# Convolution layer's input projection: twelve of sixteen channel blocks by seven half-size block products instead of eight full ones, on one Trainium2 core

## The chip, the cores and the metric

The kernel is one program on one core of a Trainium2 chip. The metric is the device time of one execution in microseconds. Five instruction streams run side by side: TensorE (PE, with its weight loads shown as PEld), VectorE (DVE), ScalarE (ACT), GpSimd (POOL) and SyncE (SP), which issues nearly all transfers.

## The reference, cut to what matters

A stack of layers on 512 tokens of width 1024 in float32: pool mixer, convolution mixer, latent attention, pool mixer, and then two blocks with attention and a feed-forward layer. The change touches the convolution mixer:

```
xn = rms_norm(x, conv_norm)                      # 512 x 1024
b, c, h, z = split(xn @ w_in, 4)                 # w_in: 1024 x 8192, so 4 parts of 2048 channels
y = b * causal_depthwise_conv(c * h, conv_w)     # width 3 along the tokens
x = x + (y * silu(z)) @ w_out                    # w_out: 2048 x 1024
```

## The kernel before, in words

**Products.** Tokens lie on the free axis, channels on the partitions. Every float32 operand is split into a high part (rounded to fp32r, by ACT) and a low part (the rest, by DVE or POOL), and each product is three matmuls: high by high, high by low, low by high (`mm3`, L454 to L456). A *unit* is a weight tile of 128x1024 for one block of 128 output channels: `gemm8` runs 8 steps of k, so 24 matmuls of 512 columns.

**Weights.** The units form one long list (`unit_table`), and every engine walks it in the same order. SP loads a unit into one of four `raw` buffers; ACT copies it to `WH` (L1133); DVE subtracts to get `WL` (L1837), or POOL does, in pieces of 256 columns (L2707), where the unit's last field says so; TensorE then multiplies. `WH` and `WL` are rings of three, so ACT can write unit n only when TensorE is done with unit n-3. The calls `weights(n)` and `taking(key)` in each engine's program fix where in its order of work this split takes place; `taking` goes two units ahead (`LOOK = 2`). All orders are written out by hand; a queue waits at each `wait_ge` with everything behind it.

**Convolution.** `conv_layer` exists in each engine's program and loops over 16 blocks of 128 channels. A block has four units, cc, ch, cb and cz (c, h, b and z). DVE scales c by 1/rms squared (L1968) and multiplies by h (L1974); ACT makes the first tap (L1251), DVE the two others (L1978, L1981), POOL multiplies by 1/rms (L2759); DVE multiplies b (L1988) and scales z (L1866); ACT takes silu (L1257), POOL multiplies it in (L2764), ACT and DVE split the result into `YH` and `YL` (L1142, L1845). After 8 blocks an output projection of 8 units follows (`out_proj("co", ...)`). The position angles for the later attention (DVE, L2032 to L2050) and their sines (ACT) lie in blocks 1 to 5.

**Other work that is named later.** The feed-forward layers at the end already use a seven-product scheme, in `quarter`, from which the names Q1 to Q7 and W5 come. `v_part` in the attention has matmuls of 256 columns.

Of the kernel before, what the change touches and what calls it, by code (L numbers as in the profile page):

```python
# [15 lines left out]
S = 512  # L16
# [55 lines left out]

FF_ORDER = (0, 4, 1, 5, 2, 6, 3, 7)
# [12 lines left out]
SEMS = ("xin0", "xin1", "xin2", "xin3", "xin4", "xin5", "xin6", "xin7", "consts", "vec", "raw0", "raw1", "raw2", "raw3", "pos", "lam", "cos", "sin", "fn", "out",  # L86
# [48 lines left out]
def unit_table(D):  # L135

    units, index, lows = [], {}, False

    def add(key, src, ncol, dup=False):
        index[key] = len(units)  # L140
        units.append([src, ncol, dup])
# [22 lines left out]
    for i2 in range(8):  # L164
        for i in (2 * i2, 2 * i2 + 1):
            for off, nm in ((16, "cc"), (32, "ch"), (0, "cb"), (48, "cz")):
                add((nm, i), D["conv_in"][0, off + i], 1024)
        if i2 % 4 == 3:
            out_units("co", D["conv_out"], i2 // 4)
# [28 lines left out]
    for l in range(2):  # L198
# [10 lines left out]
        for qd in range(4):  # L209
            for i in FF_ORDER:  # L210
                add(("f1", l, qd, i), D[f"ff1{l}"][0, qd * 8 + i], 1024)
                if qd == 0 and i == 0:
                    low(False)
            for name in PRODUCTS:
                for kk in range(2):
                    add(("zq", 4 * l + qd, name, kk), (4 * l + qd, name, kk), 1024)
    for n, u in enumerate(units):
        on = False
        for at, now in flips:
            if at + (0 if now else 0) <= max(n - LOOK, 0):  # L220
                on = now
        u.append(on)
    loaded = [n for n, u in enumerate(units) if not isinstance(u[0], tuple)]
    slots = {n: (i % NRAW, loaded[i - NRAW] if i >= NRAW else None) for i, n in enumerate(loaded)}
    return units, index, slots
# [75 lines left out]
def program(nc, D, out):  # L301
    ctx = ExitStack()
    with ctx:
# [26 lines left out]
        raw = [sb(f"raw{i}", WN) for i in range(NRAW)]  # L330
# [18 lines left out]
        units, unit, slots = unit_table(D)  # L349
# [63 lines left out]
        def weight_source(n):  # L413
            src, ncol = units[n][0:2]
            if isinstance(src, tuple):
# [15 lines left out]
        def pe_program(handle, c):  # L431
# [146 lines left out]

            def conv_layer():
                for i2 in range(8):  # L580
                    for i in (2 * i2, 2 * i2 + 1):
                        xgemm(1, "cc", i, first=i == 0)
# [530 lines left out]
        def act_program(handle, c):  # L1113
# [127 lines left out]
            def conv_layer(done):  # L1241
                for i2 in range(8):
                    for i in (2 * i2, 2 * i2 + 1):
                        taking("cc", i)
                        if i == 0:
                            root(1, 1024)
                        taking("ch", i)
                        act.wait_ge(*at("ch", i))
                        if i > 1:
                            act.wait_ge(*at("cb", i - 2))  # L1250
                        act.do.activation(CV[i % 2], temp("ch", i), ACT.Copy, scale=vcol("conv_w2", i)).then_inc(  # L1251
                            *mark("act", ("cv2", i)))
                        taking("cb", i)
                        taking("cz", i)
                        t = temp("cz", i)
                        act.wait_ge(*at("czr", i))
                        act.do.activation(t, t, ACT.Silu).then_inc(*mark("act", ("czs", i)))  # L1257
                        y_high("co", i // 8, i % 8, t, ("czy", i))
                        if i == 5:
                            sines()  # L1260
                    if i2 % 4 == 3:
                        out_proj("co", i2 // 4, done if i2 == 7 else None)

# [548 lines left out]
        def dve_program(handle, c):  # L1812
# [64 lines left out]
            def out_proj(name, rb, st=None, first=0):  # L1877
                for m in range(first, 8):
                    taking(name, rb, m)
                    add_out(m, (name, rb, m), ("x", name, rb, m) if st is None else ("x", st, m))  # L1880
                    if st is not None and st != "mid" and st < 8:
# [76 lines left out]
            def conv_layer():  # L1958
                for i2 in range(8):
                    for i in (2 * i2, 2 * i2 + 1):  # L1960
                        taking("cc", i)
                        if i == 0:
                            recip_root(1, R[:, :])
                            dve.wait_ge(*mine())
                            dve.do.tensor_tensor(CR2, R[:, :], R[:, :], ALU.mult).then_inc(*mark("dve", ("r2",)))
                        dve.wait_ge(*at("mm", "cc", i))
# [9 lines left out]
                        a = CV[i % 2]  # L1976
                        dve.wait_ge(*at("cv2", i))
                        dve.do.scalar_tensor_tensor(a, shifted(("ch", i), 1), vcol("conv_w1", i), a, ALU.mult,  # L1978
                                                    ALU.add).then_inc(*mark("dve"))
                        dve.wait_ge(*mine())  # L1980
                        dve.do.scalar_tensor_tensor(a, shifted(("ch", i), 2), vcol("conv_w0", i), a, ALU.mult,  # L1981
                                                    ALU.add).then_inc(*mark("dve", ("cv0", i), ("tfree", "ch", i)))
                        taking("cb", i)
                        dve.wait_ge(*at("mm", "cb", i))
                        dve.wait_ge(*at("cv", i))
                        if i > 1:
# [6 lines left out]
                        low(YL[i % 8][:, :], t, YH[i % 8][:, :], ("yh", "co", i // 8, i % 8),  # L1993
                            ("yl", "co", i // 8, i % 8), ("tfree", "cz", i))
                        if i == 1:
                            positions()
                        if i == 2:
                            angle("sin", SIN[:, :], 0.0, 0.0)
                        if i == 3:
                            angle("cos", COS[:, :], 0.25, math.pi / 2)  # L2000
                    if i2 % 4 == 3:
                        out_proj("co", i2 // 4, 2 if i2 == 7 else None)
# [677 lines left out]
        def pool_program(handle, c):  # L2680
# [72 lines left out]
            def conv_layer():  # L2753
                for i2 in range(8):
                    for i in (2 * i2, 2 * i2 + 1):
                        taking("ch", i)
                        pool.wait_ge(*at("cv0", i))
                        pool.wait_ge(*at("rstd", 1))
                        pool.do.tensor_tensor(CV[i % 2], CV[i % 2], R[:, :], ALU.mult).then_inc(*mark("pool", ("cv", i)))  # L2759
                        taking("cz", i)  # L2760
                        t = temp("cz", i)
                        pool.wait_ge(*at("czs", i))
                        pool.wait_ge(*at("cb", i))
                        pool.do.tensor_tensor(t, t, CB[i % 2], ALU.mult).then_inc(*mark("pool", ("czy", i)))  # L2764
                        if i == 6:
                            pool.wait_ge(*at("sin"))
                            pool.do.tensor_scalar(SIN[:, :], SIN[:, :], const[:, C_SGN:C_SGN + 1], None,
                                                  ALU.mult).then_inc(*mark("pool", ("sinr",)))
                    if i2 % 4 == 3:
# [374 lines left out]
```

## Time and profile before

| | |
|---|---|
| Time, median of 3 runs | 2676.91 us (2676.52 to 2676.93) |
| The profiled execution | 2678.12 us, of which the span of the core is 2676.3 |
| Granted TensorE clock, mean | 0.998 |
| TensorE busy | 2652.0 us, 99% of the span |
| DVE, ACT, POOL busy | 64%, 48%, 24% |
| The convolution layer | from 315.9 us, blocks of 21.8 us; the first output projection is issued from 462.3 |

The page gives busy time over the whole program. TensorE being busy in nearly all of it says that the other engines are hidden now; how much room each has is to be read in the stretch that is changed.

### The profile page before, as it was taken

How to read it: one execution, taken by the hardware profiler on the slowest of the kernel's cores; microseconds unless marked ns; L12 is line 12 of the kernel's file. 1: busy time of each engine (PE TensorE's matmuls, PEld its weight loads, DVE VectorE, ACT ScalarE, POOL GpSimd, SP SyncE). 2: the span in 40 equal slices, each digit the busy share in tenths (PEclk: the TensorE clock that was granted, in tenths of full speed). 3: DMA queues.
4: the chain of work that ended last, by engine and by line, in shares of the span. 5: the costliest groups of instructions: out<-in, count | busy, mean ns of one | idle time of the engine just before them, and what ended most of it. 6: DMA issues, size and time to landing. Idle time of an engine off the chain costs nothing.

```text
span 2676.3 us, 32512 instructions
## 1 busy us (share of the span) xinstructions
PE 2652.0 (99%) x12772; PEld 2222.6 (83%) x12772; DVE 1703.9 (64%) x2604; ACT 1272.0 (48%) x2002; POOL 651.6 (24%) x688
## 2 busy tenths in 40 slices
PE   8999999999999999999999999999999999999998
PEld 7888888888888888888888888788888888788887
DVE  7656554344466646666574768776677468776677
ACT  4323332222346636533235677654445677654445
POOL 1000111011126626500003744420000554420000
PEclk9999999999999999999999999999999999999999
DMA  4222222222221222222222221354551221255540
GB/s 161 98 99 98 90 103 102 95 95 95 96 68 63 68 88 66 79 87 105 95 100 97 79 72 40 105 141 148 173 158 42 80 64 48 97 152 153 173 142 32
DMA packets 76841, 263.98 MB, mean 99 GB/s; under 512 B 8976, under 2 KB 11536, under 8 KB 76688
## 3 DMA queue, kind: packets, MB, share of 16 engines
q1 hardware_dynamic: 71568, 245.12, 26.7%
q0 software_dynamic: 5120, 16.78, 3.7%
q8 instruction: 101, 1.65, 0.2%
q14 instruction: 52, 0.43, 0.0%
HBM read 259.77 MB, written 2.10 MB: 98 GB/s over the span
## 4 chain that ended last, share of the span: by engine, by line
PE 91%; DVE 4%; ACT 2%; POOL 2%; issue 0%; DMA 0%; SPq 0%; ACTq 0%; DVEq 0%
PE ps L454 27%; PE ps L455 26%; PE ps L456 26%; PE ps L460 2%; PE ps L459 2%; PE ps L461 2%; POOL wl L2707 2%; PE ps L595 1%; PE ps L857 1%; PE ps L856 1%; DVE wl L1837 1%; ACT wh L1133 0%; DVE xl L1849 0%; PE ps L528 0%; ACT xh L1144 0%
## 5 line engine op out<-in xcount | busy, mean ns | idle before, releaser
L454 PE MATMUL ps<-xh,wh 128*128 128x512 f32 x1920 | 752.2, 392 | 0.1
L455 PE MATMUL ps<-xl,wh 128*128 128x512 f32 x1920 | 748.1, 390 | 0.0
L456 PE MATMUL ps<-xh,wl 128*128 128x512 f32 x1920 | 748.0, 390 | 0.0
L1133 ACT ACTIVATE wh<-raw 128x1024 fp32r<-128x1024 f32 (+3 forms) x389 | 397.6, 1023 | 474.4 <-PE ps L456 434.9
L454 PEld LDWEIGHTS ps<-xh,wh 128*128 128x128 f32 x1920 | 361.0, 188 | 77.0 <-issue 1.2
L456 PEld LDWEIGHTS ps<-xh,wl 128*128 128x128 f32 x1920 | 360.9, 188 | 75.3
L455 PEld LDWEIGHTS ps<-xl,wh 128*128 128x128 f32 x1920 | 361.0, 188 | 74.7 <-issue 1.0
L1837 DVE TENSOR_TENSOR wl<-raw,wh 128x1024 fp32r<-128x1024 f32 (+1 forms) x275 | 339.6, 1235 | 119.9 <-ACT wh L1133 119.9
L2707 POOL TENSOR_TENSOR wl<-raw,wh 128x256 fp32r<-128x256 f32 x408 | 315.3, 806 | 405.5 <-ACT wh L1133 405.5
L454 PE MATMUL ps<-yh,wh 128*128 128x512 f32 x640 | 251.1, 392 | 1.5 <-POOL wl L2707 1.5
L456 PE MATMUL ps<-yh,wl 128*128 128x512 f32 x640 | 249.2, 389 | 0.0
L455 PE MATMUL ps<-yl,wh 128*128 128x512 f32 x640 | 249.1, 389 | 0.0
L2716 POOL TENSOR_TENSOR acc<-acc,t 128x512 f32<-128x512 f32 x52 | 72.9, 1403 | 679.7 <-ACT t L1154 677.4
L1133 ACT ACTIVATE wh<-a 128x1024 fp32r<-128x1024 f32 x96 | 101.9, 1062 | 126.8 <-PE ps L456 64.4
L1845 DVE TENSOR_TENSOR yl<-t,yh 128x512 fp32r<-128x512 f32 (+1 forms) x148 | 101.5, 687 | 78.2 <-ACT yh L1142 78.2
L454 PEld LDWEIGHTS ps<-yh,wh 128*128 128x128 f32 x640 | 120.2, 188 | 28.6 <-POOL wl L2707 3.2
L456 PEld LDWEIGHTS ps<-yh,wl 128*128 128x128 f32 x640 | 120.1, 188 | 25.2
L1142 ACT ACTIVATE yh<-t 128x512 fp32r<-128x512 f32 (+1 forms) x148 | 86.4, 585 | 114.3 <-DVE t L1949 56.3
L455 PEld LDWEIGHTS ps<-yl,wh 128*128 128x128 f32 x640 | 120.2, 188 | 23.9
L1874 DVE TENSOR_TENSOR x<-ps,x 128x512 f32<-128x512 f32 x96 | 65.6, 688 | 116.9 <-PE ps L456 116.9
L1837 DVE TENSOR_TENSOR wl<-a,wh 128x1024 fp32r<-128x1024 f32 x96 | 117.3, 1221 | 32.1 <-ACT wh L1133 32.1
L2827 POOL DMA_DIRECT2D wsum<-in_ff2t x32 | 27.2, 976 | 328.7 <-DMA wsum<-in_ff2t 322.8
(307 smaller groups left out, 4755.3 us busy)
## 6 DMA issues: line engine op xcount, KB each, us to landing
raw<-in_pool_in SPq DMA_DIRECT2D x64, 512.0 KB, 3.2
raw<-in_conv_in SPq DMA_DIRECT2D x64, 512.0 KB, 3.2
raw<-in_ff SPq DMA_DIRECT2D x64, 512.0 KB, 6.2
a<-in_ff2t SPq DMA_DIRECT2D x64, 512.0 KB, 6.9
raw<-in_pool_out SPq DMA_DIRECT2D x32, 512.0 KB, 3.2
raw<-in_qk SPq DMA_DIRECT2D x32, 512.0 KB, 3.5
raw<-in_pool_grp SPq DMA_DIRECT2D x16, 512.0 KB, 3.2
raw<-in_conv_out SPq DMA_DIRECT2D x16, 512.0 KB, 3.2
```

Source lines behind the costliest of these rows:

```text
L454: pe.do.matmul(o, lh, rh_, start=start, stop=False)
L455: pe.do.matmul(o, lh, rl_, start=False, stop=False)
L456: return pe.do.matmul(o, ll, rh_, start=False, stop=stop)
L459: pe.do.matmul(o, lh, rh_, start=False, stop=False, skip_group_check=True)
L460: pe.do.matmul(o, lh, rl_, start=False, stop=False, skip_group_check=True)
L1133: act.do.activation(h[:, 0:ncol], r[:, 0:ncol], ACT.Copy).then_inc(*mark("whi", ("whi", k)))
L1142: act.do.activation(dst, src, ACT.Copy).then_inc(*mark("act", done))
L1837: dve.do.tensor_tensor(lo[:, 0:ncol], r[:, 0:ncol], f(h[:, 0:ncol]), ALU.subtract).then_inc(*mark("wlo", ("wlo", k)))
L1845: dve.do.tensor_tensor(dst, src, f(h), ALU.subtract).then_inc(*mark("dve", *done))
L1874: dve.do.tensor_tensor(x[m][:, :], ps(*key)[:, :], x[m][:, :], ALU.add).then_inc(*mark("dve", ("psfree",) + key, *done))
L2707: p = pool.do.tensor_tensor(lo[:, cc], r[:, cc], f(h[:, cc]), ALU.subtract)
L2716: pool.do.tensor_tensor(ACC[:, :], ACC[:, :], temp("sq", use, k), ALU.add).then_inc(*mark("pool", ("acc", use, k), ("tfree", "sq", use, k)))
```

## The change

Blocks 2 to 6 and 8 to 14 (`CONV_BLOCKS`) are computed by `conv_part` instead of four calls of `gemm8`. The four projections of a block form two pairs, (c, h) and (b, z). The input is halved along k and along the tokens, a pair's weights are halved along k, and the 2x2 block product takes seven products of half size: each has 4 steps of k with three matmuls of 256 columns, 12 matmuls. The seven are grouped into four units for each pair (`CONV_PARTS`): three of 1024 columns with two products and one of 512 with one. The units of the pairs alternate: U0 = (pair 0, part 0), U1 = (pair 1, part 0), U2, ... U7. Of the weights only part 0 and part 3 are loaded; the middle parts are four sums of 512 columns that POOL makes (`w_sums`), for block i+1 while block i runs. Four sums of the inputs for each of four k are made once, by POOL, ACT and DVE, in blocks 0 and 1 (`x_scaled`, `t_sums`, `t_high`, `t_low`). Partial sums leave PSUM through ACT and DVE (`first_sum`, `second_sums`, `third_sum`, `upper`, `lower`). The low half of part 3 (U6 and U7) is made by POOL. The rest of a block's elementwise work moves to the next block's order. Two more raw buffers are used from block 3 on. The angles move into the first output projection, the sines behind it.

```diff
+CONV_BLOCKS = (2, 3, 4, 5, 6, 8, 9, 10, 11, 12, 13, 14)
+CONV_PAIRS = ((16, 32), (0, 48))
+CONV_PARTS = (("Q1", "Q2"), ("Q6", "W5"), ("Q7", "Q3"), ("Q4",))
...
+    tails = {index["cp", i, p, 3] for i in CONV_BLOCKS for p in range(2)}
...
-        u.append(on)
+        u.append(on or n in tails)
...
+            def conv_part(i, p, j):
+                n = unit["cp", i, p, j]
+                wh, wl = unit_ready(n)
...
+                for c, name in enumerate(CONV_PARTS[j]):
...
+                    for k in range(4):
...
+                            mm = mm3(o, wh[:, cc], wl[:, cc], xh, xl, k == 0, k == 3)
```

ACT's part of `conv_layer`:

```diff
+                def x_scaled(k):
+                    if k:
+                        act.wait_ge(*at("tcs", k - 1))
+                    for dst, m in ((COS, k), (SIN, k + 4)):
+                        act.wait_ge(*at("x", 1, m))
+                        a = act.do.activation(dst[:, :], x[m][:, :], ACT.Copy, scale=vcol("conv_norm", m))
...
+                def t_high(k):
+                    if k == 0:
+                        act.wait_ge(*at("mm", "grp", 0, 3, 3))
+                    high(TC[k][:, 0:1024], RX[k % 2][:, :], ("tcs", k), ("tch", k))
...
+                def eight(i):
...
+                    if i == 1:
+                        t_high(1)
+                        x_scaled(2)
+                    taking("ch", i)
...
+                    tap(i)
+                    if i == 1:
+                        t_high(2)
+                        x_scaled(3)
+                    taking("cb", i)
+                    if i == 0:
+                        x_scaled(0)
+                    taking("cz", i)
+                    if i == 0:
+                        t_high(0)
+                        x_scaled(1)
+                    if i == 1:
+                        t_high(3)
+                    gate(i)
+                    y_out(i)
```

DVE's part:

```diff
+                def seven(i):
+                    late = i - 1 in CONV_BLOCKS
+                    for s in range(8):
+                        if late and s == 0:
+                            lower(i - 1, 1, 1)
+                            lower(i - 1, 1, 0)
+                        if late and s == 1:
+                            taps(i - 1)
+                        if late and s == 2:
+                            gated(i - 1)
+                        if s == 5:
+                            third_sum(i, 0)
+                            upper(i, 0)
+                            both_scaled(i)
+                        if s == 6:
+                            third_sum(i, 1)
+                            lower(i, 0, 1)
+                        if s == 7:
+                            lower(i, 0, 0)
+                            upper(i, 1)
+                        weights(unit["cp", i, s % 2, s // 2] + LOOK)
+                        if late and s == 4:
+                            y_out(i - 1)
```

POOL's part:

```diff
+                def w_sums(i, p):
...
+                    pool.do.tensor_tensor(s1, b[:, 0:512], b[:, 512:1024], ALU.add).then_inc(
+                        *mark("pool", ("ws1", i, p)))
...
+                    if before is not None:
+                        pool.wait_ge(*at("wlo", unit["cp", before, p, 2]))
+                    pool.do.tensor_tensor(s3, a[:, 0:512], b[:, 0:512], ALU.add)
+                    pool.wait_ge(*at("ws1", i, p))
+                    pool.do.tensor_tensor(s2, s1, a[:, 0:512], ALU.add).then_inc(*mark("pool", ("ws", i, p, 0)))
+                    pool.wait_ge(*at("ws", i, p, 0))
+                    pool.do.tensor_tensor(s4, s2, a[:, 512:1024], ALU.add).then_inc(*mark("pool", ("ws", i, p, 1)))
+
+                for i in range(16):
+                    if i - 1 in CONV_BLOCKS:
+                        taps(i - 1)
+                        gated(i - 1)
+                    if i not in CONV_BLOCKS:
+                        taps(i)
+                    if i < 2:
+                        t_sums(2 * i)
+                    if i == 1:
+                        t_sums(3)
+                    if i not in CONV_BLOCKS:
+                        gated(i)
+                    if i == 0:
+                        t_sums(1)
+                    if i + 1 in CONV_BLOCKS:
+                        w_sums(i + 1, 0)
+                        if i in CONV_BLOCKS:
+                            weights(unit["cp", i, 1, 3])
+                        w_sums(i + 1, 1)
+                    elif i in CONV_BLOCKS:
+                        weights(unit["cp", i, 1, 3])
```

`t_sums(k)` is five POOL operations of 256 columns. `taps` on POOL is the product by 1/rms, `gated` on POOL the product with silu(z), both of 512 columns. On DVE `taps` is two operations of 512 columns with both inputs in SBUF; `both_scaled`, `gated` and `y_out` are one such operation each, `lower` with half 1 is one of 256 columns; `third_sum`, `upper` and `lower` with half 0 read one input from PSUM.

## Rows read from the trace of the kernel before

**Rows 1.** The page: busy time of each engine, and the chain that ended last.
```profile
PE 2652.0 (99%) x12772; PEld 2222.6 (83%) x12772; DVE 1703.9 (64%) x2604; ACT 1272.0 (48%) x2002; POOL 651.6 (24%) x688
...
PE 91%; DVE 4%; ACT 2%; POOL 2%; issue 0%; DMA 0%; SPq 0%; ACTq 0%; DVEq 0%
```

**Rows 2.** One block's stretch: length; busy PE, PEld, DVE, ACT, POOL; granted clock, DMA.
```profile
425.40:447.20 21.80, 21.80 (x97) 18.05 (x97) 9.69 (x12) 6.01 (x7) 3.50 (x2) 1.00 0.26 97
```

**Rows 3.** Timeline of TensorE: start, duration; 256 columns, then 512.
```profile
1475.90 0.28 PE L456 MATMUL ps<-wh,xl 128*128 128x256 f32 x1
...
1476.14 0.28 PE L455 MATMUL ps<-wl,xh 128*128 128x256 f32 x1
...
1479.13 0.39 PE L454 MATMUL ps<-xh,wh 128*128 128x512 f32 x1
...
1479.81 0.39 PE L454 MATMUL ps<-xh,wh 128*128 128x512 f32 x1
```

**Rows 4.** Groups of instructions from 330 to 462 us: busy, mean ns | idle before.
```profile
L1837 DVE TENSOR_TENSOR wl<-raw,wh 128x1024 fp32r<-128x1024 f32 x26 | 31.7, 1221 | 4.0 <-ACT wh L1133 4.0
L1133 ACT ACTIVATE wh<-raw 128x1024 fp32r<-128x1024 f32 x25 | 26.2, 1052 | 20.0 <-PE ps L456 19.9
...
L2764 POOL TENSOR_TENSOR t<-t,s 128x512 f32<-128x512 f32 x6 | 7.8, 1292 | 37.7 <-ACT t L1257 37.7
L1981 DVE SCALAR_TENSOR_TENSOR s<-t,vec,s 128x512 f32<-128x512 f32 x7 | 5.3, 752 | 0.2
...
L1251 ACT ACTIVATE s<-t,vec 128x512 f32<-128x512 f32 x7 | 5.1, 724 | 36.5 <-DVE t L1974 36.5
```

**Rows 5.** Line L2759 alone: duration in ns, least, median, most.
```profile
L2759 POOL TENSOR_TENSOR s<-s,r x16: 2202/2211/2220, 335.2 to 700.5; 128x512 f32<-128x512 f32 x16
```

**Rows 6.** Timeline of DVE and POOL, four stretches: start, duration of the run.
```profile
418.00 1.22 DVE L1837 TENSOR_TENSOR wl<-raw,wh 128x1024 fp32r<-128x1024 f32 x1
418.16 2.22 POOL L2759 TENSOR_TENSOR s<-s,r 128x512 f32<-128x512 f32 x1 [11.76 <-DVE s L1981]
...
23.31 4.54 DVE L1837 TENSOR_TENSOR wl<-raw,wh 128x1024 fp32r<-128x1024 f32 x2 [3.00 <-ACT wh L1133]
24.68 4.33 POOL L2716 TENSOR_TENSOR acc<-acc,t 128x512 f32<-128x512 f32 x2
...
2328.80 4.44 POOL L2707 TENSOR_TENSOR wl<-raw,wh 128x256 fp32r<-128x256 f32 x5
2328.83 2.40 DVE L1849 SCALAR_TENSOR_TENSOR xl<-x,vec,xh 128x512 fp32r<-128x512 f32 x2
...
1501.46 0.68 DVE L2300 SCALAR_TENSOR_TENSOR s<-ps,s 128x512 f32<-128x512 f32 x1
...
1501.64 2.83 POOL L2707 TENSOR_TENSOR wl<-raw,wh 128x256 fp32r<-128x256 f32 x4
...
1504.44 1.29 POOL L2835 TENSOR_TENSOR x<-x,s 128x512 f32<-128x512 f32 x1
...
1505.69 2.82 POOL L2707 TENSOR_TENSOR wl<-raw,wh 128x256 fp32r<-128x256 f32 x4
```

**Rows 7.** Line L1845 with its operands in SBUF: least, median, most ns.
```profile
L1845 DVE TENSOR_TENSOR ptl<-s,pth x96: 539/558/7402, 1502.8 to 2318.9; 128x384 fp32r<-128x384 f32 x64, 128x512 fp32r<-128x512 f32 x32
```

**Rows 8.** Timelines of ACT in block 0 and of DVE in block 1.
```profile
333.43 1.99 ACT L1133 ACTIVATE wh<-raw 128x1024 fp32r<-128x1024 f32 x2
335.44 1.28 ACT L1257 ACT_TABLE_LOAD   x1
339.95 0.63 ACT L1257 ACTIVATE t<-t 128x512 f32<-128x512 f32 x1 [3.23 <-DVE t L1866]
...
349.28 0.69 DVE L1974 TENSOR_TENSOR t<-ps,s 128x512 f32<-128x512 f32 x1 [2.71 <-PE ps L456]
```

**Rows 9.** Stretches of 2 us, later in the program, with the granted clock.
```profile
1624.00:1626.00 2.00, 1.48 (x10) 1.48 (x11) 1.22 (x3) 1.94 (x5) 0.00 (x0) 1.00 0.01 4
...
1628.00:1630.00 2.00, 2.00 (x13) 1.59 (x12) 1.97 (x8) 2.00 (x6) 0.00 (x0) 0.50 0.00 0
```

More of the change, by code:

```diff
@@ L135, in unit_table, with add @@
 def unit_table(D):
-    units, index, lows = [], {}, False
-    def add(key, src, ncol, dup=False):
+    units, index, loads, wide, narrow = [], {}, [], [], []
+    def add(key, src, ncol, dup=False, load=True):
         index[key] = len(units)
+        if load and not isinstance(src, tuple):
+            loads.append(len(units))
         units.append([src, ncol, dup])
@@ L221, in unit_table @@
                 on = now
-        u.append(on)
-    loaded = [n for n, u in enumerate(units) if not isinstance(u[0], tuple)]
-    slots = {n: (i % NRAW, loaded[i - NRAW] if i >= NRAW else None) for i, n in enumerate(loaded)}
-    return units, index, slots
+        u.append(on or n in tails)
+    queue, holder, slots = list(range(NRAW)), {}, {}
+    for i, n in enumerate(loads):
+        if i in wide:
+            queue = [NRAW, NRAW + 1] + queue
+        if i in narrow:
+            queue = [q for q in queue if q < NRAW]
+        q = queue.pop(0)
+        queue.append(q)
+        slots[n] = q, holder.get(q)
+        holder[q] = n
+    return units, index, slots, loads
 def temp_table():
@@ L1253, in conv_layer @@
[L1253 to L1260, printed above, removed]
+                        if i in CONV_BLOCKS:
+                            seven(i)
+                        else:
+                            eight(i)
@@ new lines, in gated, with seven @@
+                def gated(i):
+                    o = CB[i % 2]
+                    dve.wait_ge(*at("cup", i, 1))
+                    dve.wait_ge(*at("cv", i))
+                    dve.do.tensor_tensor(o, o, CV[i % 2], ALU.mult).then_inc(*mark("dve", ("cb", i)))
+                def seven(i):
+                    late = i - 1 in CONV_BLOCKS
+                    for s in range(8):
+                        if late and s == 0:
+                            lower(i - 1, 1, 1)
+                            lower(i - 1, 1, 0)
+                        if late and s == 1:
+                            taps(i - 1)
[11 more added lines that the diff above has]
+                            upper(i, 1)
+                        weights(unit["cp", i, s % 2, s // 2] + LOOK)
+                        if late and s == 4:
+                            y_out(i - 1)
@@ L1959, in conv_layer @@
                 for i2 in range(8):
                     for i in (2 * i2, 2 * i2 + 1):
+                        if i in CONV_BLOCKS:
+                            seven(i)
+                            continue
+                        late = i - 1 in CONV_BLOCKS
                         taking("cc", i)
```

272 lines of the change are left out of this document (221 added, 51 removed).

## The prediction

> **What bounds the kernel now.** The page comes first: TensorE is busy in 2652.0 of 2676.3 us and holds 91% of the chain that ended last [rows 1], so time goes only where TensorE's work or its waits change. Next, the stretch of one convolution block, since the mean over the program says nothing of it: 21.8 us with TensorE busy throughout at the full clock (1.00), DVE busy 9.7, ACT 6.0, POOL 3.5 [rows 2]. Then TensorE's timeline for the price of a matmul, the groups for the other engines' prices, and last the timelines of DVE and POOL together. These last matter most, since the change gives POOL about five times its work there.
>
> **What TensorE gains.** A matmul of 512 columns starts 0.227 us after the one before, one of 256 columns 0.120 us [rows 3]. A block had 96 of the first (21.76 us) and gets 2 x 7 x 12 = 168 of the second (20.16 us). That is 1.6 us, and 19.2 us over twelve blocks: seven eighths of the columns, of which gain the fixed 13 ns of each matmul, now paid 168 times, takes back nearly half. The same sums are accumulated in PSUM, and transfers stay at four of 512 KB for a block; six raw buffers instead of four put them ahead, so I cost them at nothing.
>
> **What the other engines get, for each full block.** ACT: six splits of 1.05 us [rows 4], two half ones, six small copies and the three operations of before, about 12 us, hidden. DVE: six low halves of 1.22 us [rows 4] and eleven smaller operations, about 15 us. POOL: its two products of 512 columns, eight sums of 512 in `w_sums`, four pieces of 256 for U6 and U7. POOL's price is 1.29 us alone for 512 columns [rows 4], 1.25 from start to start in a run, and 0.70 for a piece of 256 [rows 6]: 10 x 1.25 + 4 x 0.70 = 15.3 us, with the wait for DVE's `gated` between POOL's two products (0.7) and small waits on its own results 16.4 us (0.4 for these, an estimate). Alone, this would fit under 20.16.
>
> **But the two do not run alone.** When DVE has two inputs in SBUF, it and POOL take turns. L2759, 512 columns like L2764 (1.29 us), takes 2.20 to 2.22 in all 16 blocks [rows 5], because DVE's low half has started 0.16 us before it [rows 6]. In runs, DVE's 1024 columns and POOL's 512 go pairwise at 2.2 us, which is nearly the sum of both alone; two DVE operations of 512 lengthen five POOL pieces from 3.5 to 4.44 us, 0.45 each [rows 6]. With one input in PSUM DVE is not slowed though POOL is at work (0.68 us) [rows 6]. So each of DVE's operations with two SBUF inputs lengthens POOL's chain: a low half by 0.92 (2.21 - 1.29), 512 columns by 0.45, 256 by about 0.2. In a block these are six low halves (5.5), two taps, `both_scaled` and `y_out` (1.8; `gated` falls in POOL's wait), and two `lower` (0.4): 7.7 us. POOL's round becomes 16.4 + 7.7 = 24.1 us, 3.9 more than TensorE's 20.16. The Trainium skill ("SBUF — State Buffer", section "Who interferes with whom") states this rule: a DVE instruction with two SBUF inputs contends with a GpSimd one that reads SBUF, whoever comes first blocks the other fully, and one with a single SBUF input does not contend. By that rule, the trace agrees (2.21 against 1.29 us), the change loses what its fewer products gain.
>
> Does TensorE wait for this round? POOL's order is `taps`, `gated`, `w_sums` pair 0, U6 and U7, `w_sums` pair 1, all in one queue. U6 and U7 stand behind the first sums, and TensorE can't finish a block without them; next block's `taps` stand behind the second sums, and DVE's `gated` and POOL's `gated` behind these. So the round sets the period from the second block of a run on. The last block of a run makes no sums for the next and the first block of the second run has its sums made under the output projection: I count no excess for blocks 6, 8 and 14. Blocks 3, 4, 5 and 9 to 13 pay 3.9 each, 31 us. Bounds: with holds only and no idle time, POOL has 12 and DVE 9 units of about 1.15 and 1.05 us, 23.2 us, excess 25 in all. If only half of DVE's operations met POOL's, the round would be 20.3 and the excess nothing. Upward, 26.5 us a round (51 in all) if turns go badly: one DVE operation of 0.56 us took 7.4 [rows 7], through POOL's whole run of ten from 1501.64 to 1509.8 [rows 6]. I take the sum of rows, since turns are the rule in them.
>
> **The entry.** In blocks 0 and 1 the sums of the inputs are made by a relay through in-order queues. One `t_sums` is five pieces of 256 columns, 3.9 us with waits on itself; one `t_high` 1.06; one `x_scaled` two operations, 1.4; a unit's split 1.05 + 1.22 with hops, 2.4 [rows 4, 6]. Times are on the clock of before, where ch of block 1 is done at 349.2 (DVE reads it at 349.28 [rows 8]); with units of 5.44 us block 1 starts at 338.3 and block 2 at 360.1.
> (1) ACT in block 0: after its two splits (333.43 on [rows 8]) and `x_scaled` it waits for `t_sums(0)`, which starts when L2759 ends (335.2 + 2.2 = 337.4 [rows 5]) and ends at 342.2 with one turn lost; `t_high(0)`, `x_scaled(1)`, the table load of 1.28 us and the silu [rows 8] end at 346.6 instead of 340.6. POOL's product, ACT's `y_out`, then cb's split: ready 350.9, wanted 349.2. Stall 1.7.
> (2) `t_sums(1)` from 348.0 to 353; `t_high(1)`, `x_scaled(2)`, cz's split: 357.5, wanted 356.3. Stall about 1.
> (3) DVE's product for ch stands behind that low half; then ACT's tap, DVE's taps, POOL's `taps` (2.2), only then `t_sums(2)`, `t_high(2)`, `x_scaled(3)` and U0's split, since ACT's `taking("cb")` is behind them: about 371.5, wanted 362.5. Stall 9.
> (4) `t_sums(3)`, `t_high(3)`, silu, POOL's product, three sums of `w_sums(2, 0)`, U2's split: 383.4, wanted 377.2. Stall 6.
> (5) Four more sums with one turn lost, U3's split: stall 3.
> Together 21 us. Bounds: 10 (steps 3 and 4 half as long, because some of it overlaps) and 26. I keep 21: every step is a queue that is written down.
>
> Smaller moves: the angles (7 us of DVE) go under an output projection in which DVE has little to do; blocks 7 and 15 are as before; nothing for either. A low granted clock is seen once, 0.50 from about 1627 on, right after 2 us in which TensorE was busy only 1.48 [rows 9]. The stalls forecast here are longer, so the clock may fall behind each; where POOL's round sets the period the slower matmuls fill time that TensorE would wait in, so I add nothing and widen the upper end.
>
> **Sum.** -19.2 + 31 + 21 = +33 us against the profiled execution's own 2678.1 (span 2676.3), the same edit of the same stretch as against the median 2676.9, which is 1.2 lower. Forecast 2710 us.
>
> **Rivals.**
> A. The turns are mostly missed, because DVE's and POOL's bursts fall apart in time: TensorE sets the period in all twelve blocks, and the entry, less its lost turns, is 10 to 15 us. Then -19.2 + 10 to 15: 2667 to 2673, faster. For it: the block has 20 us and POOL alone needs 16.4. Against: 15.3 us of POOL and some 9.5 of DVE's two-input work (9 times 1.05) don't fit in 20.16 without meeting. It decides if the measured round is under 20.5 us.
> B. Starved DVE: runs of three to five sums without a gap keep DVE out as in the 7.4 us case, and DVE's low halves come late as well; the clock halves. Rounds of 27 to 28: 8 x 7.5 = 60, entry 26: 2740 to 2750. For it that one case; against it, the median of the same line is 0.56 us and the pairs in [rows 6] take turns at the first boundary.
> C. The change doesn't do what it says: 256 columns don't go at 0.120 us when weights and inputs change this way. At 0.1295 us a block of 168 costs 21.76 again, the gain of 19.2 is gone in blocks 2, 6, 8 and 14 (6.4 us), and the others wait anyway: 2716. Against: the same widths run at 0.120 in `v_part` [rows 3].
>
> **Chances.** Forecast with its own range 2692 to 2732: 0.68, C included. A: 0.17, of which 0.13 faster and 0.04 within 0.2%. B: 0.10. The rest, 0.05, lies between A and the forecast. 0.2% is 5.4 us, about what a measurement of this kernel can tell. The range takes in the lower bounds of both terms (-19.2 + 25 + 10: 2693, and halfway to A) and most of the way to B: 2680 to 2742. Faster 0.13, same 0.06, slower 0.81.
>
> **What would show it.** The convolution's blocks on TensorE: 20.2 us in blocks 6, 8 and 14; about 24 in 4, 5 and 10 to 13, with the wait before U6 or U7 and released by POOL's L2707-like low half. POOL busy nearly all of a block, its sums at 1.25 to 2.2 us each instead of 1.29. TensorE waits of about 9 and 6 us around 362 and 377 us, released by low halves that follow ACT. Matmuls of 256 columns at 0.120 us apart. Wrong if POOL's operations keep 1.29 us while DVE works, if the waits in full blocks are under 1 us, or if the entry's relay overlaps more than the queues let me see.

## The result, and the profile after

The changed kernel takes 2727.11 us (median of 4 runs, 2724.9 to 2729.25) against 2676.92 for the kernel before, run beside it: a ratio of 1.0187, 95% interval 1.017 to 1.0205. The profiled execution has a span of 2726.5 us against 2676.3, so 50.2 us have to be found. The page of the kernel after, busy time by engine and then the chain that ended last, beside [rows 1]:

```profile
PE 2654.7 (97%) x13636; PEld 2265.7 (83%) x13636; DVE 1820.4 (67%) x2704; ACT 1343.8 (49%) x2134; POOL 877.2 (32%) x852
...
PE 82%; POOL 7%; DVE 6%; ACT 3%; issue 1%; DMA 0%; SPq 0%; POOLq 0%; ACTq 0%; DVEq 0%
```

TensorE's share of the chain has fallen from 91% to 82%, POOL's has risen from 2% to 7%. The end of block 1 (first line), blocks 2 to 6 and block 8, beside [rows 2] (same columns), say where:

```profile
352.00:372.20 20.20, 11.52 (x49) 8.89 (x49) 6.90 (x9) 8.13 (x10) 10.01 (x11) 0.91 0.15 52
372.20:409.90 37.70, 26.21 (x169) 25.51 (x170) 18.62 (x19) 11.96 (x18) 29.44 (x23) 0.78 0.23 80
409.90:433.90 24.00, 22.08 (x171) 21.61 (x170) 18.90 (x20) 11.46 (x17) 20.36 (x14) 0.93 0.26 90
433.90:460.30 26.40, 22.67 (x170) 22.47 (x169) 19.27 (x20) 11.26 (x17) 22.68 (x17) 0.88 0.28 86
460.30:483.20 22.90, 20.81 (x170) 20.40 (x169) 16.98 (x20) 11.47 (x17) 18.67 (x13) 0.99 0.22 73
483.20:503.40 20.20, 20.20 (x171) 20.20 (x170) 17.84 (x19) 10.87 (x16) 14.10 (x9) 1.00 0.37 126
568.90:589.05 20.15, 20.15 (x169) 20.15 (x168) 10.41 (x13) 9.71 (x14) 12.19 (x10) 1.00 0.21 68
```

Blocks 6 and 8 (the last two lines), in which TensorE waits for nothing, take 20.2 us, as computed. Block 2 takes 37.7; blocks 3, 4 and 5 take 24.0, 26.4 and 22.9; blocks 9 to 13, by the starts of their first matmuls, 26.25, 26.09, 22.91, 26.11 and 26.1. Over 20.16 each that is 12.85 + 26.7 = 39.5 us. The entry (blocks 0 to 2) is 12.1 us to the start of block 2 and 17.5 in it, 29.6. With -19.2 for the matmuls the sum is 49.9 of the 50.2 measured.

TensorE's longest waits up to block 4, from its timeline, the last figure in brackets being the idle time and what ended it:

```profile
372.17 0.58 PE L490 MATMUL ps<-xh,wh 128*128 128x256 f32 x1 [8.17 <-DVE wl L1998]
...
386.31 0.58 PE L495 MATMUL ps<-tc,wh 128*128 128x256 f32 x1 [6.77 <-DVE wl L1998]
...
405.41 0.39 PE L495 MATMUL ps<-tc,wh 128*128 128x256 f32 x1 [4.17 <-POOL wl L2959]
...
429.23 0.39 PE L495 MATMUL ps<-tc,wh 128*128 128x256 f32 x1 [1.92 <-POOL wl L2959]
...
455.05 0.58 PE L495 MATMUL ps<-tc,wh 128*128 128x256 f32 x1 [3.73 <-POOL wl L2959]
```

The first two, before block 2 and before its U2, stand in the entry. The other three are at U6 of blocks 2, 3 and 4, all ended by POOL's low half. Where the first matmul lasts 0.58 us instead of 0.39, the granted clock is already at its lower level: it is 0.50 for 3.4 to 10.2 us at nine of TensorE's waits in the layer.

POOL's round, from its timeline (the lines of the kernel after: L3009 is `taps`, L3015 `gated`, L3041 to L3050 `w_sums`, L2959 the low halves of U6 and U7):

```profile
415.51 2.21 POOL L3009 TENSOR_TENSOR s<-s,r 128x512 f32<-128x512 f32 x1 [2.61 <-DVE s L2128]
418.59 2.15 POOL L3015 TENSOR_TENSOR t<-t,s 128x512 f32<-128x512 f32 x1 [0.87 <-DVE s L2175]
420.69 2.27 POOL L3041 TENSOR_TENSOR sw<-raw 128x512 f32<-128x512 f32 x1
...
440.31 2.21 POOL L3009 TENSOR_TENSOR s<-s,r 128x512 f32<-128x512 f32 x1 [2.61 <-DVE s L2128]
```

24.8 us from one `taps` to the next; the eight blocks 3 to 5 and 9 to 13 last 25.1 in the mean. The products and sums of 512 columns that take 1.29 us alone [rows 4] have means of 1.49 to 2.21 us in these groups, the costliest of the stretch from 410 to 484 us:

```profile
L3048 POOL TENSOR_TENSOR sw<-sw,raw 128x512 f32<-128x512 f32 x4 | 8.0, 2011 | 0.0
...
L3041 POOL TENSOR_TENSOR sw<-raw 128x512 f32<-128x512 f32 x4 | 7.1, 1774 | 0.0
L3009 POOL TENSOR_TENSOR s<-s,r 128x512 f32<-128x512 f32 x3 | 6.6, 2212 | 8.5 <-DVE s L2128 8.5
L3015 POOL TENSOR_TENSOR t<-t,s 128x512 f32<-128x512 f32 x3 | 6.4, 2145 | 2.6 <-DVE s L2175 2.6
L3050 POOL TENSOR_TENSOR sw<-sw,raw 128x512 f32<-128x512 f32 x4 | 6.0, 1492 | 0.3
```

That is three rounds. The last two numbers of L3009 and L3015 matter as much: POOL stands idle (8.5 + 2.6) / 3 = 3.7 us a round, waiting for DVE. An engine that idles 3.7 us of 25 doesn't set a period by its own queue. The chain of waits shows what does: a ring, in which each step releases the next and the last one releases the first step of the next round (start, duration, what):

```profile
455.05 0.58 PE ps L495
...
458.07 1.07 ACT wh L1210
...
459.16 2.00 DVE wl L1998
461.16 1.43 DVE t L2163
...
462.92 1.13 DVE wl L1998
...
464.75 0.77 DVE s L2128
...
465.59 2.23 POOL s L3009
...
467.84 0.70 DVE s L2175
...
468.68 1.04 POOL t L3015
...
470.79 2.27 POOL sw L3041
...
477.72 3.93 POOL wl L2959 x4
```

U6 on TensorE gives a `WH` buffer back, ACT can then split the second unit of the next block, DVE makes its low half, the two `lower`, the low half of U2 and the taps, all ahead of POOL's `taps`; POOL's sums follow, and behind them the low half of the next U6. POOL's second sums run beside DVE's part of this ring, and what they have left over is POOL's idle time.

### The profile page after: what moved, and what is told of

The parts are those of the page before. It is cut to its first block, busy times and chain, and to the rows that moved or that the text cites. A ratio compares the mean times of both kernels' runs of the same rounds, so it can differ in the third digit from the quotient of the medians.

```text
span 2726.5 us, 34706 instructions
## 1 busy us (share of the span) xinstructions
PE 2654.7 (97%) x13636; PEld 2265.7 (83%) x13636; DVE 1820.4 (67%) x2704; ACT 1343.8 (49%) x2134; POOL 877.2 (32%) x852
## 3 DMA queue, kind: packets, MB, share of 16 engines
q8 instruction: 108, 1.77, 0.3%
## 4 chain that ended last, share of the span: by engine, by line
PE 82%; POOL 7%; DVE 6%; ACT 3%; issue 1%; DMA 0%; SPq 0%; POOLq 0%; ACTq 0%; DVEq 0%
PE ps L490 23%; PE ps L491 23%; PE ps L492 23%; PE ps L495 3%; PE ps L497 3%; PE ps L496 3%; POOL wl L2959 2%; DVE wl L1998 2%; PE ps L672 1%; POOL sw L3041 1%; ACT wh L1210 1%; POOL s L3009 1%; POOL sw L3048 1%; POOL sw L3046 1%; POOL sw L3050 1%
## 5 line engine op out<-in xcount | busy, mean ns | idle before, releaser
L490 PE MATMUL ps<-xh,wh 128*128 128x512 f32 (+1 forms) x1728 | 658.3, 381 | 10.9 <-DVE wl L1998 10.8
L491 PE MATMUL ps<-xl,wh 128*128 128x512 f32 (+1 forms) x1728 | 653.5, 378 | 0.0
L492 PE MATMUL ps<-xh,wl 128*128 128x512 f32 (+1 forms) x1728 | 653.2, 378 | 0.0
L1210 ACT ACTIVATE wh<-raw 128x1024 fp32r<-128x1024 f32 (+3 forms) x369 | 369.8, 1003 | 468.0 <-PE ps L492 364.5
L2959 POOL TENSOR_TENSOR wl<-raw,wh 128x256 fp32r<-128x256 f32 x440 | 344.9, 816 | 410.1 <-ACT wh L1210 410.0
L490 PEld LDWEIGHTS ps<-xh,wh 128*128 128x128 f32 x1728 | 326.7, 189 | 73.9 <-DVE wl L1998 12.0
L1998 DVE TENSOR_TENSOR wl<-raw,wh 128x1024 fp32r<-128x1024 f32 x239 | 305.5, 1279 | 122.3 <-ACT wh L1210 121.0
L492 PEld LDWEIGHTS ps<-xh,wl 128*128 128x128 f32 x1728 | 326.2, 189 | 60.5
L491 PEld LDWEIGHTS ps<-xl,wh 128*128 128x128 f32 x1728 | 326.7, 189 | 59.5 <-issue 1.0
L2006 DVE TENSOR_TENSOR yl<-t,yh 128x512 fp32r<-128x512 f32 (+1 forms) x148 | 108.6, 735 | 54.0 <-ACT yh L1219 54.0
L1219 ACT ACTIVATE yh<-t 128x512 fp32r<-128x512 f32 (+1 forms) x148 | 86.3, 585 | 112.3 <-DVE t L2112 56.4
```

The lines of the kernel that those rows point to most:

```text
L490: pe.do.matmul(o, lh, rh_, start=start, stop=False)
L491: pe.do.matmul(o, lh, rl_, start=False, stop=False)
L492: return pe.do.matmul(o, ll, rh_, start=False, stop=stop)
L1210: act.do.activation(h[:, 0:ncol], r[:, 0:ncol], ACT.Copy).then_inc(*mark("whi", ("whi", k)))
L1219: act.do.activation(dst, src, ACT.Copy).then_inc(*mark("act", done))
L1998: dve.do.tensor_tensor(lo[:, 0:ncol], r[:, 0:ncol], f(h[:, 0:ncol]), ALU.subtract).then_inc(*mark("wlo", ("wlo", k)))
```

## The experiments

**1. Take the turns away.** DVE's low halves of U0 to U5 read a spare PSUM bank instead of the raw weights or sums, so that DVE has one SBUF input. The true low halves are left out.

```diff
+                    elif k in conv_units:
+                        for c0 in (0, 512):
+                            p = dve.do.tensor_tensor(lo[:, c0:c0 + 512], PS[SPARE][:, :], f(h[:, c0:c0 + 512]),
+                                                     ALU.subtract)
```

> Changed computation: in blocks of seven products DVE's low half of U0 to U5 subtracts from a PSUM bank that nobody writes in place of the raw weights, in two operations of 512 columns, so DVE's time stays (2 x 0.61 against 1.22 us) and only one input is in SBUF. Theory 1 (turns between DVE and POOL): the round of POOL loses 5.5 us, from about 25 to 19.5, TensorE sets the period of 20.2 us in blocks 3 to 5 and 9 to 13, and their waits before U6 or U7 (0.9 to 4.6 us) vanish with the clock's drops behind them: about 40 us less, 2687 us; POOL's sums go at 1.25 to 1.3 us. Theory 2 (POOL's own work and the order of its queue are too long, whoever runs beside it): unchanged, 2727 us.

Measured: 2683.17 us (2681.92 to 2683.89), ratio 1.002 (1.0011 to 1.003). The same groups of POOL as above, in this kernel:

```profile
L3020 POOL TENSOR_TENSOR s<-s,r 128x512 f32<-128x512 f32 x4 | 5.2, 1306 | 10.6 <-DVE s L2139 10.6
L3026 POOL TENSOR_TENSOR t<-t,s 128x512 f32<-128x512 f32 x4 | 5.2, 1300 | 3.5 <-DVE s L2186 3.5
...
L3052 POOL TENSOR_TENSOR sw<-raw 128x512 f32<-128x512 f32 x4 | 5.2, 1295 | 0.0
```

POOL's operations of 512 columns are back at 1.29 to 1.33 us in the mean (these three took 2.21, 2.15 and 1.77 in the kernel after), POOL has exactly as many operations in the whole program (852), blocks 3 to 5 and 9 to 13 take 20.16 us, and 44 us are gone. DVE's own work has not become shorter than it was alone: a low half is 2 x 0.68 us, against 1.22 for the real one outside a turn. The turns between DVE and POOL are the cause of the rounds. What is left is the entry, 11.7 us ahead of block 2 and 33.9 - 20.16 = 13.7 in it, less the 19.2: 6.2 us, and the spans differ by 5.0.

**2. Make the sums once.** POOL makes the weight sums of block 2 only; later blocks use them again, so their own sums are left out.

```diff
                 def w_sums(i, p):
+                    if i != CONV_BLOCKS[0]:
+                        return
```

> Changed computation: POOL makes the sums of the weights for block 2 alone and all later blocks use these, so eight POOL operations of 512 columns are left out in each of ten blocks. Theory 1 and theory 2 both: POOL's round falls by more than 10 us, blocks 3 to 5 and 9 to 13 run at 20.2 us, 2687 us, and what is left over 2657.7 (2676.9 - 19.2) is the entry, about 29 us with block 2. A rival in which the seven-product blocks are held by ACT, by DVE's own sums or by transfers: still 24 to 26 us a block.

Measured: 2682.14 us (2679.41 to 2682.7), ratio 1.0017 (1.0007 to 1.0026). Blocks at 20.16 again, though POOL's two products still take 2.21 and 2.15 us. So turns alone cost nothing; they cost where POOL has eight sums a block to make in them. Block 2 takes 31.8 us here: without sums for block 3 its wait before U6 is gone.

**3. DVE makes the low halves of U6 and U7.** This part of the change undone.

```diff
-        u.append(on or n in tails)
+        u.append(on)
```

> The low halves of U6 and U7 go back to DVE, all else is kept. By turns: POOL's chain loses 2.8 us and meets two more DVE operations of 512 columns (0.9), so the round falls by about 1.9, eight times, and with fewer drops of the clock some 20 us in all: about 2707 us. TensorE's wait then moves from U6 to the middle units, whose sums come last. Rival: the second part of the title is what makes the block fit (DVE is the fuller engine): slower than 2727, by the 0.6 us of each DVE operation that delays U0's low half, 5 to 15 us.

Measured: 2710.18 us (2708.64 to 2711.93), ratio 1.0122 (1.0107 to 1.0137). The round is 23.43 us. Giving these low halves to POOL costs 17 us instead of sparing any: they stand in POOL's part of the ring. POOL's idle time a round is now 3.28 + 0.87 us. Of the 17 us 4.3 are in block 2, and the granted clock, which falls at six waits in the rounds of the kernel after, falls at none here, so not all of the rest is POOL's work. The size was as expected, the place of TensorE's waits was not: they are before U7 and before U0, not at the middle units.

```profile
448.81 0.35 PE L495 MATMUL ps<-tc,wh 128*128 128x256 f32 x1 [1.24 <-DVE t L2142]
452.02 0.39 PE L490 MATMUL ps<-xh,wh 128*128 128x256 f32 x1 [1.54 <-DVE wl L1998]
```

**4. Fill TensorE's wait.** 20 matmuls of 256 columns on data at hand, ahead of U6, keep TensorE at work while it waits, so that the clock isn't lowered.

```diff
+                if j == 3 and p == 0 and i + 1 in CONV_BLOCKS:
+                    b = bank("fill", i)
+                    for r in range(FILL):
+                        mm = pe.do.matmul(b[:, 0:256], XH[0][:, 0:128], XH[0][:, 0:256], start=r == 0, stop=r == FILL - 1)
```

> Added work: 20 matmuls of 256 columns (2.4 us) into a spare bank in front of U6 in blocks 2 to 5 and 8 to 13, where TensorE waits. Theory 1 with the clock as a cost of its own: the waits are shorter, the clock falls less often, and time falls by up to 10 us (six drops of 1.7 to 2.7 us each). Rival, the prediction's own statement that slow matmuls only fill time that POOL's round takes anyway: unchanged within 3 us, or slower by up to 24 us if TensorE has no room for them (2.4 us in each of ten blocks).

Measured: 2726.63 us (2725.98 to 2727.34), ratio 1.0183 (1.0168 to 1.0199). The convolution has five stretches of low clock instead of nine, only one of them in a round. In the chain U6 now takes 1.7 us of TensorE instead of 2.9 (its matmuls follow each other at 0.12 us instead of 0.21), yet from `taps` to `taps` the round is 24.8 us instead of 25.0: DVE's first tap, further on in the ring, meets POOL and takes 1.71 us instead of 0.68. The unchanged time hides two effects, though. The eight blocks last 24.4 us in the mean instead of 25.1, 5.3 us less together, while block 8, in which TensorE waits for nothing, is 2.4 us longer by the added matmuls (20.15 in the kernel after):

```profile
569.17:591.73 22.56, 22.56 (x190) 22.55 (x188) 11.22 (x14) 9.84 (x15) 14.52 (x12) 1.00 0.27 89
```

So the low clock costs up to 5.3 us of the 39.5 in the rounds, and not nothing. The ring itself gains little of this; 2.8 us of it are in block 13, the last before a block without a wait.

**5. Start at block 3.** `CONV_BLOCKS` without 2, so eleven blocks, the input sums still in blocks 0 and 1.

> Block 2 goes back to four full products, the relay of input sums in blocks 0 and 1 stays. If the entry is made of in-order queues as the prediction counts them: the three waits of 2.7, 0.7 and 8.6 us before block 2 stay (they come from ACT's weight splits behind x_scaled), while those in block 2 (7.1, 1.0 and 4.5 us) shrink to some 8 us in block 3, since the sums of its weights start behind POOL's last product of block 2. 2676.9 - 17.6 + 12 + 8 + 2 x 5 + 26.5 = 2716 us. Rival, the entry is the first use of the sums and moves with the first block: all waits move on by one block and only one round of 5 us is saved, 2722 to 2724.

Measured: 2719.27 us (2718.5 to 2722.38), ratio 1.0157 (1.0142 to 1.0172), between the two, nearer the first. The waits ahead of 372 us stay as they were (2.69, 0.67 and 8.56 from matmul to matmul), and the first block of seven products still has waits, of 3.95 us at U2, 1.72 at U3 and 3.33 at U6 (against 7.05, 0.96 and 4.45 in the kernel after). Part of the entry follows the first block, part belongs to the input sums.

**6. Spread the entry.** Full blocks 0 to 3, one `t_sums` in each, and POOL's operations put so that none stands ahead of a split which TensorE needs; seven products in ten blocks.

```diff
-CONV_BLOCKS = (2, 3, 4, 5, 6, 8, 9, 10, 11, 12, 13, 14)
+CONV_BLOCKS = (4, 5, 6, 8, 9, 10, 11, 12, 13, 14)
...
+                        if i < 3:
+                            t_sums(i)
```

> One input sum for each of blocks 0 to 3, none in front of a weight split that TensorE is about to want; sums of weights for block 4 made before POOL's products of block 3; seven products in blocks 4 to 6 and 8 to 14. By the queues, the entry is gone (0 to 3 us) and what is left is the rounds: 2676.9 - 16 + 5 (block 5) + 26.5 (blocks 9 to 13), 2692 to 2695 us. Rival, the first block of a run is slow by itself whatever the order: 10 to 17 us more, 2702 to 2710.

Measured: 2699.47 us (2697.53 to 2700.3), ratio 1.0082 (1.0065 to 1.0099). TensorE waits for nothing before 412 us: the waits ahead of the first block came from where the input sums stood, and went when these were moved and spread over four blocks. Then come 4.6 us before U2 of block 4, which takes 26.7 us, and the rounds as before, six of them (24.0 to 26.8 us, and 23.0 once). The time lies between the two expectations, since the first block is still 6.5 us too long.

**7. Alternate.** The same with a full block between each two of seven products, so that POOL's sums for one are made in the full block before it.

```diff
-CONV_BLOCKS = (4, 5, 6, 8, 9, 10, 11, 12, 13, 14)
+CONV_BLOCKS = (4, 6, 8, 10, 12, 14)
```

> As the spread kernel, with seven products only in blocks 4, 6, 8, 10, 12 and 14, so that POOL's sums for a block are made in the full block before it and its round lasts 20.2 + 21.8 us. Theory of turns: POOL has about 30 us of work with turns in 42, TensorE sets both periods, 6 x 1.6 = 9.6 us less than before, 2667 us (ratio 0.9964). Rival, the order (not the amount) of POOL's and DVE's work holds TensorE: waits of 1 to 2 us in each pair, 2673 to 2680 us.

Measured: 2703.02 us (2702.74 to 2705.23), ratio 1.0096 (1.0081 to 1.0111): a miss by 36 us. In blocks 6, 10, 12 and 14 TensorE waits 0.65 us before U0 and 4.07 before U2, in block 4 4.34 before U2, in block 8, behind the output projection, not at all. The wait of 4.07 comes this way (timelines of POOL, ACT and TensorE):

```profile
458.23 1.26 POOL L3006 TENSOR_TENSOR t<-t,s 128x512 f32<-128x512 f32 x1
```

```profile
459.53 0.63 ACT L1219 ACTIVATE yh<-t 128x512 fp32r<-128x512 f32 x1 [3.76 <-POOL t L3006]
460.06 1.04 ACT L1210 ACTIVATE wh<-sw 128x1024 fp32r<-128x1024 f32 x1
```

```profile
462.42 0.58 PE L495 MATMUL ps<-tc,wh 128*128 128x256 f32 x1 [4.07 <-DVE wl L1993]
```

The full block's `y_out` (L1219) waits on ACT for POOL's `gated`, which stands behind the sums (451.15 to 458.2), and U2's split is queued behind it. Nothing needs `y_out` before the output projection.

**8. The same, low halves of U6 and U7 by DVE.** The edit of 3 on the kernel of 7.

> As the alternate kernel, with the low halves of U6 and U7 by DVE. Theory: neither engine is full, so it makes no difference unless DVE then reaches U0's low half late, as it does by 1.8 us a block where full runs have DVE make them: 0 to 6 x 1 us above the alternate kernel, 2667 to 2673.

Measured: 2702.89 us (2702.32 to 2704.12), ratio 1.0095 (1.008 to 1.011), the same as 7, so the 17 us of experiment 3 appear only where blocks of seven products follow each other. The level was missed for 7's reason: the waits are 7's, 0.65 and 4.08 us.

**9. `y_out` behind the splits.** The kernel of 7 with the full block's `y_out` after the fifth split of the next block, on ACT and DVE, and DVE's `gated` ahead of the product with h.

```diff
-                        if late and s == 4:
+                        if i != 8 and s == 4:
                             y_out(i - 1)
...
-                    y_out(i)
+                    if i + 1 not in CONV_BLOCKS or i == 7:
+                        y_out(i)
```

> The alternate kernel with two moves. ACT's and DVE's last step of a full block (y_out) goes behind the weight splits of the seven-product block after it, since in the alternate kernel ACT's split of U2 stood behind y_out, that behind POOL's gated, and that behind the second sums of the weights (4.35 us of TensorE's wait a pair, and the clock at half behind it). DVE's gated goes ahead of the product for h, since POOL had waited 6.2 us for it. If these queues were the cause, TensorE sets both periods: 6 x 1.6 less than before, with 0 to 3 us of small waits: 2668 to 2671 us (ratio 0.9964 to 0.9975). Rival, turns between DVE and POOL hold the pair whatever the order: waits of 2 us and more in every pair remain, 2680 us or more.

Measured: 2668.96 us (2666.37 to 2670.23, 7 runs) against 2676.68, ratio 0.9971 (0.996 to 0.9983): faster than both kernels, by 0.3% of the time, and the only version here that is. A full block and one of seven products, by windows:

```profile
423.60:445.40 21.80, 21.80 (x98) 18.08 (x98) 16.76 (x18) 6.74 (x8) 13.54 (x9) 1.00 0.47 169
445.40:465.60 20.20, 20.20 (x170) 20.16 (x170) 11.95 (x14) 10.63 (x16) 9.32 (x8) 1.00 0.21 78
```

TensorE waits nowhere in the layer, though DVE and POOL are both well filled in the full block (16.8 and 13.5 us). The second output projection starts at 698.86 us instead of 708.12 in the kernel before: 9.3 us earlier, for 6 x 1.6 = 9.6 expected. What each of the two moves brings alone was not tried.

**10. One sum earlier.** POOL's first sum for the next block ahead of `taps`, into its idle time.

```diff
+                    if early:
+                        w_first(i + 1, 0)
                     if i - 1 in CONV_BLOCKS:
                         taps(i - 1)
```

> The changed kernel, with POOL's first sum for the next block (pair 0) ahead of its product taps instead of behind gated, in blocks 3 to 5 and 9 to 13. In the changed kernel POOL stands idle for 1.4 to 3.3 us before taps, because DVE's taps are late. If the round is held by the way tail, U7, ACT and DVE, taps, gated, sums, tail, one sum of 1.25 to 2.3 us leaves that way and fills the idle time: some 1 us a round, 8 us in all, 2719 us. Rival, POOL's total of work and turns holds the round and its idle time is slack: unchanged, 2727 us.

Measured: 2722.5 us (2721.73 to 2724.0), ratio 1.0173 (1.0159 to 1.0186): 4.6 us less (3.7 by the ratios), 0.6 a round. The moved sum takes 1.67 us in a turn with DVE, and `taps` still waits 0.63. POOL's sums of pair 0 now take 5.3 us instead of 7.1, but the low halves of U6 and U7 behind them 4.4 instead of 3.8, and DVE's part of the ring meets the moved sum: most of the gain comes back in other links.

**11 and 12. The order of four loads.** The profile after has one more wait that no step of the prediction holds, the 4.17 us before U6 of block 2. POOL and then SP's queue ahead of it:

```profile
389.94 1.28 POOL L3050 TENSOR_TENSOR sw<-sw,raw 128x512 f32<-128x512 f32 x1
397.38 1.29 POOL L3041 TENSOR_TENSOR sw<-rx 128x512 f32<-128x512 f32 x1 [6.16 <-DMA rx<-in_conv_in]
```

```profile
385.27 6.35 SPq L3245 DMA_DIRECT2D raw<-in_conv_in  x2
391.67 0.90 SPq L3245 DMA_DIRECT2D rx<-in_conv_in  x2
```

SP issues block 3's first two units into the buffers that POOL's sums of block 2 give back (until 385.2 and 391.2), and only then the last two, which go to the two new buffers, free since about 378.6; POOL's first sum needs one of these. The edit issues the last two first, in the kernel after (11) and in that of experiment 1 (12).

```diff
+    a = loads.index(index["cp", CONV_BLOCKS[1], 0, 0])
+    loads[a:a + 4] = loads[a + 2:a + 4] + loads[a:a + 2]
```

> The kernel after, with the last two loads of block 3 (into the two buffers added by the change) issued ahead of its first two; every load goes to the same buffer as before, only their order in SyncE's queue is changed. In the kernel after GpSimd stands idle 6.16 us at 391.2 for the load of one of these buffers, whose issue at 391.67 stood in SyncE's queue behind two loads that wait for GpSimd's own sums of block 2 (ends at 385.2 and 391.2), and TensorE then waits 4.17 us before U6 of block 2, with 3.4 us of the lower clock behind it. Theory (the wait is that of the load order, a transfer cost that the prediction put at nothing): GpSimd's idle 6.16 us shrinks below 1 us, TensorE's 4.17 us wait and the 1.7 us lost to the clock behind it go, 4 to 6 us in all: 2721 to 2723, ratio about 1.0168. Rival (GpSimd's rounds take it back: it then only waits longer for DVE's taps at the start of block 3's round): the wait before U6 goes, but block 3 starts its round no earlier, 2725 to 2727.

> The same change of order, in the first experiment's kernel (low halves from PSUM, no turns, blocks 3 and later at 20.16 us, 2683.2 us). There GpSimd waits 5.78 us for the same load and TensorE 2.8 us before U6 of block 2. Theory: the wait and the lower clock behind it go: 2678.5 to 2680, ratio about 1.0007. Since no round of GpSimd sets the period there, nothing can be given back; if the time stays at 2683, the load order is not what makes U6 late.

Measured: 12 takes 2679.44 us (2676.77 to 2680.6, 11 runs), ratio 1.0005 (0.9996 to 1.0014), 3.7 less than experiment 1; block 2 29.4 us instead of 33.9. 11 takes 2724.87 (2724.01 to 2725.8), ratio 1.0176 (1.0162 to 1.019), 2.2 less than the kernel after (3 by the ratios) and so between the two expectations; the two kernels' times overlap, but the profiles agree: block 6 ends 2.4 us earlier. Its loads and sums:

```profile
378.85 0.81 SPq L3247 DMA_DIRECT2D rx<-in_conv_in  x2
```

```profile
391.42 2.29 POOL L3043 TENSOR_TENSOR sw<-rx 128x512 f32<-128x512 f32 x1
394.93 2.14 POOL L3048 TENSOR_TENSOR sw<-raw,rx 128x512 f32<-128x512 f32 x1 [1.23 <-DVE wl L2000]
```

POOL's wait for the load is gone in both, and TensorE's wait behind it is 0.28 us in 11 and nothing in 12. Where TensorE sets the period the gain stays. In 11 block 2 is 5.4 us shorter (32.3), but POOL's `taps` of the next round starts only 2.8 us earlier, TensorE waits 4.50 us before U6 of block 3 instead of 1.92, and block 3 is 3.1 us longer (27.1).

## Why the prediction was right, and where its terms were off

Slower, 2710 in the range 2680 to 2742, was right, and by the mechanism named; the size was 17 us short.

- **TensorE's gain, -19.2.** Right: 20.15 to 20.2 us in blocks 6 and 8, matmuls 0.120 us apart, and 9.3 us for 6 x 1.6 in experiment 9. Only the side remark is off that the fixed 13 ns take back nearly half of the gain: 72 more matmuls cost 0.94 us of 2.57, over a third.
- **The turns.** The cause is right: `taps` at 2.212 us as in [rows 5], POOL back at 1.30 us and the rounds gone in experiment 1. The Trainium skill ("SBUF — State Buffer", section "Who interferes with whom") has the rule with its exception for a single SBUF input; the trace agrees with both halves, 2.21 us with two SBUF inputs on DVE's side, 1.31 with one.
- **The round, 24.1 us.** Measured 25.1. Two terms were off against each other. "The wait for DVE's `gated` between POOL's two products (0.7)" is 0.87, but another wait stands ahead of `taps`, 8.5 / 3 = 2.8: 3.7 of idle time instead of 0.7. POOL's own work with its turns is 25.1 - 3.7 = 21.4 instead of 23.4, so the turns cost POOL about 5.7 us a round (21.4 less its own 15.3 and 0.4) and not 7.7. The prediction wrote the queue of POOL down and let it set the period; the chain shows that the ring goes through TensorE's U6, ACT's split and seven DVE operations as well. The excess was 39.5 us for 31. That the measured round lies so near the forecast one is in part luck.
- **The last of a run, no excess.** Right: 20.2 in block 6 and 20.15 in block 8; 20.2 for 14 (716.5 to 736.7).
- **The entry, 21 us.** Measured 29.6. Steps (1) to (3) came to 12.1 us for 11.7, steps (4) and (5) to 6.77 + 0.55 = 7.3 us of idle time for 9: step (4), forecast at 6, took 6.8, and step (5), forecast at 3, took 0.6. The rest of block 2 was not in the sum. "Six raw buffers instead of four put them ahead, so I cost them at nothing" failed: the new buffers' loads stand in SP's queue behind loads that wait for POOL's sums, 4.17 us. Without it block 2 is 4.5 us shorter (12 against 1), and in the kernel itself 2.2 of these reach the end (11). And TensorE is busy 26.2 us instead of 20.16 in block 2 at a clock of 0.78: 6.0 us.
- **The clock.** "I add nothing" held for the kernel's time in experiment 4 (0.5 us in all, inside the spread), but only since block 8 grew by the added matmuls: its blocks with waits were 5.3 us shorter together, so up to 5.3 of the 8.5 us by which the rounds exceeded their forecast can be the clock's. In block 2, where TensorE's own matmuls are links of the relay, the 6.0 us are in the stretch; what of them would go at the full clock was not tried.
- **The rivals.** A fell at its own condition, a round over 20.5 us; and even without turns the time would be 2683, not 2667 to 2673, as its entry of 10 to 15 us is 25 in experiment 1. B fell: no DVE operation was kept out as in [rows 7], the low halves last 1.2 to 2.3 us. C fell: 0.120 us.

What stays open is the split of the ring's 25 us among its links: each experiment that shortened one (4 and 10) saw another lengthen by a turn.

## What to carry to other kernels

Where two engines must take turns, don't add up one engine's queue: follow the ring of links through every engine, with POOL's idle time as the sign that the ring and not POOL sets the period. Price a new buffer by the place of its load in the issuing queue, not by its size: what stands ahead of it may wait for the very engine that it should feed. And a saving of TensorE's work is only had at the rate at which its helpers keep up; here half as many blocks by seven products, with the helpers' work in the blocks between and nothing optional ahead of a split, gain 7.7 us where all twelve lose 50.

## What the runs showed of the hardware

- A DVE operation with both inputs in SBUF and a POOL operation that reads SBUF take turns also in long alternation, 1024 columns against 512: up to 2.28 us for a sum of 1.29, and 1.74 to 2.32 for eight of nineteen low halves of 1.22 (kernel after, 409 to 484 us). That POOL isn't slowed at all when one DVE input comes from PSUM (means of 1.29 to 1.33 us in experiment 1) had been seen only for DVE's side [rows 6].
- The granted clock fell to 0.50 for 3.4 to 10.2 us at nine of TensorE's waits in the convolution, of 1.92 to 8.17 us. At the first, of 2.29 us at 352.2, it did not fall; in the profiles of experiments 4 and 11 it fell at that same wait (2.30 and 2.29 us), so a wait of this length can go either way.
